# Pauses, order and place: the chain of tiles 1 and 2 beside gathered expert rows in a hybrid decoder step

## The reference, cut to what matters

```
h  = modulate(rms_norm(x));  z = h @ w_in
o  = [sparse attention (compressed, selected, window) | causal pooling mixer]
x1 = x + gate1 * (o @ w_out)
h2 = modulate(rms_norm(x1))
q  = h2 @ peer_wq;  s = q . peer_subkeys        # 8 heads, two sets of 128 keys
eid, g = top16 of the 16 x 16 sums; g = softmax # 128 experts for each token
a  = gelu(h2 . peer_u[eid])
y  = x1 + gate2 * sum_k (g * a)_k peer_v[eid_k]
```

## Time and profile before

| | us |
|---|---|
| median of three runs | 2595.06 |
| the profiled execution's own time | 2596.01 |
| its span in the trace | 2594.2 |
| VectorE busy | 1758.1 (68%) |
| TensorE busy | 1273.0 (49%) |
| GpSimd busy | 1111.4 (43%) |
| ScalarE busy | 212.3 (8%) |
| first row of tile 0's dots / sums | 600.8 / 1048.9 |
| first row of tile 1's dots / sums | 1562.4 / 1902.6 |
| start of the looped phases | 2256.4 |

### The profile page before, as it was taken

How to read it: one execution, slowest core, us unless ns; L and a number is a source line. 1 busy time by engine, 2 the same in 40 slices (tenths; PEclk the granted TensorE clock), 3 DMA queues, 4 the chain that set the end, 5 groups by cost and what they waited for, 6 DMA issues and landing times.

```text
span 2594.2 us, 17761 instructions
## 1 busy us (share of the span) xinstructions
PE 1273.0 (49%) x6317; PEld 690.3 (27%) x6317; DVE 1758.1 (68%) x2243; ACT 212.3 (8%) x559; POOL 1111.4 (43%) x686
## 2 busy tenths in 40 slices
PE   4699998896680542456866961000035466200000
PEld 2363534582230531343323930000012122000000
DVE  1010112226968977996558668999999967899897
ACT  3110013100010221121001011000000000000000
POOL 1000100002434744674124312688853455788684
PEclk9699899898795555566985975555566767655555
DMA  9949899759999989999998989999999999999897
GB/s 296 329 178 422 321 420 277 225 191 382 389 419 397 378 359 347 412 411 343 338 397 319 418 310 392 355 422 422 422 401 340 349 408 416 422 422 422 368 422 302
DMA packets 163041, 944.47 MB, mean 364 GB/s; under 512 B 34635, under 2 KB 44435, under 8 KB 56830
## 3 DMA queue, kind: packets, MB, share of 16 engines
q0 software_dynamic: 94784, 682.66, 65.8%
q1 hardware_dynamic: 68175, 260.74, 28.0%
HBM read 937.36 MB, written 10.26 MB: 365 GB/s over the span
## 4 chain that ended last, share of the span: by engine, by line
DVE 25%; PE 24%; DMA 22%; POOL 16%; issue 9%; SPq 2%; ACT 1%; POOLq 0%; DVEq 0%; ACTq 0%
POOL arena L668 11%; DMA arena<-in_peer_u,arena 10%; DVE arena L1994 7%; DVE arena L1971 6%; POOL arena L680 5%; DMA arena<-in_w_out 5%; DMA arena<-in_peer_v,arena 5%; PE PS L1445 3%; PE PS L1016 3%; DMA arena<-in_w_ada 3%; PE PS L1166 2%; PE PS L966 2%; PE PS L1253 2%; PE PS L1468 2%; PE PS L1070 2%
## 5 line engine op out<-in xcount | busy, mean ns | idle before, releaser
L1971 DVE CUSTOM_DVE_ANT_0 arena<-arena 128x2048 f32<-128x2048 f32 x256 | 582.3, 2289 | 117.6 <-DMA arena<-in_peer_u,arena 116.2
L668 POOL DMA_INDIRECT arena<-in_peer_u,arena x256 | 441.3, 1724 | 475.3 <-DVE arena L1971 275.9
L1994 DVE SCALAR_TENSOR_TENSOR arena<-arena 128x2048 f32<-128x2048 f32 x226 | 530.9, 2349 | 159.8 <-DMA arena<-in_peer_v,arena 155.1
L668 POOL DMA_INDIRECT arena<-in_peer_v,arena x256 | 379.7, 1483 | 442.2 <-DVE arena L1994 329.1
L1468 PE MATMUL PS<-arena 128*128 128x512 f32 x240 | 177.7, 909 | 476.3 <-DMA arena<-in_peer_v,arena 400.7
L1468 PEld LDWEIGHTS PS<-arena 128*128 128x128 f32 x240 | 68.6, 300 | 586.1 <-issue 499.9
L1474 PE MATMUL PS<-arena 128*64 128x512 f32 x8 | 5.9, 903 | 345.7 <-DVEq L2037 345.7
L2027 DVE SCALAR_TENSOR_TENSOR arena<-arena 128x2048 f32<-128x2048 f32 x64 | 150.5, 2352 | 11.3 <-DMA arena<-in_peer_v,arena 5.6
L966 PE MATMUL PS<-arena 128*32 128x512 f32 x768 | 123.2, 741 | 69.4 <-DMA arena<-in_w_ada 66.1
L2024 DVE CUSTOM_DVE_ANT_0 arena<-arena 128x2048 f32<-128x2048 f32 x64 | 144.9, 2289 | 8.1 <-DMA arena<-in_peer_u,arena 6.3
L680 POOL DMA_INDIRECT arena<-in_peer_v,arena x64 | 132.8, 2075 | 35.2 <-issue 19.2
(11 more groups left out here) (347 smaller groups left out, 1812.7 us busy)
## 6 DMA issues: line engine op xcount, KB each, us to landing
arena<-in_w_ada SPq DMA_DIRECT2D x96, 1024.0 KB, 12.0
arena<-in_w_in SPq DMA_DIRECT2D x32, 1048.0 KB, 10.2
arena<-in_peer_wq SPq DMA_DIRECT2D x32, 1024.0 KB, 9.9
arena<-in_w_in SPq DMA_DIRECT2D x32, 768.0 KB, 11.6
arena<-in_w_out SPq DMA_DIRECT2D x16, 1024.0 KB, 30.3
arena<-in_w_out SPq DMA_DIRECT2D x32, 512.0 KB, 23.6
arena<-in_peer_u,arena POOLq DMA_INDIRECT x320, 13.9
arena<-in_peer_v,arena POOLq DMA_INDIRECT x320, 13.4
```

The costliest lines, as they stand in the source:

```text
L668: pool.indirect_dma_start(out=rows_ring[:, k % NROW, :], out_offset=None, in_=tables[kind], in_offset=bass.IndirectOffsetOnAxis(ap=ids[:, ...
L1971: V.tensor_tensor_reduce(out=buf, in0=buf, in1=h2(t), scale=1.0, scalar=0.0, op0=ALU.mult, op1=ALU.add, accum_out=dots[:, t, r:r + 1]).the ...
L1994: V.scalar_tensor_tensor(out=acc[t], in0=rows_ring[:, k % NROW, :], scalar=dots[:, t, r:r + 1], in1=acc[t], op0=ALU.mult, op1=ALU.add).the ...
```

## The change

The pauses are cut (12, 20, 3, 20, 30 become 0, 2, 3, 4, 20, and the one ahead of the second addition is three times the one ahead of the first). In `beside_dots` most other pauses between steps become one row; an attention unit has three yields in place of four. Sample attention moves from `beside_sums` into `beside_dots`, with three yields a sample in place of six. `paced(work, n)` puts n yields after each step of a generator: the second expert half of tile 1 moves into tile 0's sums (2 rows a step), the first half of tile 2 into tile 1's dots (3 rows a step), and the second half of tile 2 stays in tile 1's sums (2 rows a step). `expert_exp` takes one half at a time, and ScalarE has them at other places; `gelu(0)` goes behind sample attention and the gate's evictions. TensorE spreads the first gate for both column halves before the products of the output projection, over all eight banks, in place of one half at a time.

```diff
-Q_PAUSE, K_PAUSE, S_PAUSE, OUT_PAUSE, WQ_PAUSE = 12, 20, 3, 20, 30
+Q_PAUSE, K_PAUSE, S_PAUSE, OUT_PAUSE, WQ_PAUSE = 0, 2, 3, 4, 20
@@ ScalarE
-            def expert_exp(t):
-                for half in range(2):
-                    w = gw[:, t, half * HH:(half + 1) * HH]
-                    act.wait_ge(s_e2, 2 * t + half + 1)
-                    A(w, w, exp).then_inc(s_e2x, 1)
+            def expert_exp(t, half):
+                w = gw[:, t, half * HH:(half + 1) * HH]
+                act.wait_ge(s_e2, 2 * t + half + 1)
+                A(w, w, exp).then_inc(s_e2x, 1)
...
-            expert_exp(0)
+            expert_exp(0, 0)
...
                 A(qkr[:, 1:3, NH:24], qkr[:, 1:3, NH:24], sqrt).then_inc(s_zrt, 1)
+            expert_exp(0, 1)
...
-            gelu(0)
...
-                        A(GB_12[h][:, k, m * SECTION:(m + 1) * SECTION], PS[:, 4 + 2 * k + m, :], copy).then_inc(s_gb, 1)
+                        A(GB_12[h][:, k, m * SECTION:(m + 1) * SECTION], PS[:, 4 - 4 * h + 2 * k + m, :], copy).then_inc(s_gb, 1)
+            gelu(0)
             norm2(1)
...
             chunk_out(5)
+            expert_exp(1, 0)
...
-            expert_exp(1)
+            expert_exp(1, 1)
+            expert_exp(2, 0)
             gelu(1)
-            expert_exp(2)
+            expert_exp(2, 1)
@@ TensorE
-                        last = spread(4 + 2 * k + m, 2, 2 * h + m, selT[:, k, :])
+                        last = spread(4 - 4 * h + 2 * k + m, 2, 2 * h + m, selT[:, k, :])
                 last.then_inc(s_gp, 1)
-                if h == 1:
-                    pe.wait_ge(s_gb, 12)
+            pe.wait_ge(s_gb, 12)
+            for h in range(2):
...
-                pe.wait_ge(s_gb, 8)
@@ VectorE
+            def paced(work, n):
+                for _ in work:
+                    yield from pause(n)
@@ beside_dots
-                yield from pause(4)
+                yield
                 cmp_shift(1, 6)
-                yield from pause(2)
+                yield
...
-                yield from pause(3)
+                yield
                 cmp_norm(1)
-                yield from pause(4)
+                yield
                 p_max(8)
                 for u in range(8, 16):
                     yield
+                    p_norm(u)
                     yield
-                    p_norm(u)
                     if u < 15:
-                        yield
                         p_max(u + 1)
                     yield
-
-            def beside_sums():
-
                 yield from pause(S_PAUSE)
                 dve.wait_ge(s_bs, 32)
                 dve.wait_ge(s_gsi, 16 * NH)
                 s_max(0)
                 for b in range(DB):
-                    yield from pause(2)
+                    yield
                     smp_norm(b)
+                    yield
                     if b + 1 < DB:
-                        yield from pause(2)
                         s_max(b + 1)
-                    yield from pause(2)
+                    yield
+
+            def beside_sums():
+
                 for h in range(2):
-                    yield from pause(OUT_PAUSE)
+                    yield from pause(OUT_PAUSE * (2 * h + 1))
                     yield from add1(h)
...
                 yield from pause(WQ_PAUSE)
                 yield from experts(1, 0)
+                yield from paced(experts(1, 1), 2)
 
             def beside_dots1():
-                yield from experts(1, 1)
-                yield from pause(2)
+                yield from paced(experts(2, 0), 3)
                 shares(1)
@@ beside_sums1
-                for half in range(2):
-                    yield from experts(2, half)
+                yield from paced(experts(2, 1), 2)
                 yield from pause(2)
```

## The result

The changed kernel takes 2657.59 us (median of four runs, 2652.2 to 2665.52) against 2595.11 us: a ratio of 1.0241, 95% interval 1.0223 to 1.0259, 62.5 us slower. I had forecast 2621, 26 us slower, with a range of 2573 to 2658. The sign was right; the loss was 2.4 times the one forecast.

The account below looks back on a forecast made before the run. DMA queues bound the kernel wherever VectorE keeps up. Losing 32 us through sample attention and 34 to tile 0's end, regaining 40 in tile 1, gave 26 us: 2621, own range 2603 to 2640, with rivals 2573 to 2658.

Parts of the forecast that it names:

- 92 MB of other loads: All loads behind 600 us other than the gathered rows, sized by their shapes: 219 us at 422 GB/s.
- Gain 1: ScalarE's new order removes TensorE's 46.0 us wait before the input projection's second half; it ends at 726, not 768.7.
- Loss 1: Up to the attention units: VectorE waits 13 and 6.6 us; units start at 800 after 41 rows, not 884 after 80.
- Loss 2: Attention units with three rows, not four: 9.9 us each, DMA idling some 19 us in 24 rows.
- Loss 3: Sample attention: late biases and pages, then steps with nothing spare; it ends at 1014 with 95 rows, 32 us lost.
- first-page wait: Start of sample attention: VectorE waits about 20 us because the first value pages queue behind two pieces of w_out.
- a ring of 13.5: Sample attention: each sample's chain of dependent steps across engines takes 13.5 us, against 9.3 us of VectorE work.
- the rows hide the ring: Rival in sample attention: a sample goes at VectorE's 9.3 us and the first wait goes; 2578 us, chance 0.27.
- the pages set it: Rival in sample attention: page loads make each sample 18.7 us in place of 13.5; +36, 2657 us, chance 0.15.
- To the end of tile 0's sums: From sample attention's end to tile 1's dots: a further 34 us lost, dots starting at 1628, 66 us later.
- Gains 2 and 3: Fewer expert steps beside tile 1: dots 325 us against 340, sums 329 against 354, together 40 us back.
- The sum: Whole kernel: 32 + 34 - 40 = 26 us slower, 2621 us against 2595.1.

Follow-up runs that it names:

- a_win100: Changed kernel with the large copy (win_sample, 3968 KB) left at row 100 and the small one (pool_sample, 224 KB) issued at row 300: 2651.10 us.

## Why the prediction was right or wrong

**The step that failed** is "the output projection's loads share the queues with 34 rows in 155 us; after it is the same, so they end at 1169 with row 129". They ended at 1189 with row 128. The term was mis-sized: from the end of sample attention to the last product it took 183 us (1006 to 1189), not 155, and only that sample attention ended 8 us ahead of my 1014 hides a part of it. I took the stage's duration from the trace of before and left out what else stands on POOL's queue: 4.3 MB of copies, tied to row 100 and not to the stage. My 92 MB of other loads lack them too (the trace has 96.7 MB beside the rows behind 600 us). The change moved row 100 from the attention units to the start of this stage. Without the copies there, the products take 142 to 145 us; the time falls by 22 us with the copies at row 300 or on SyncE's queue, and by 31 with them at row 88. The prediction's remark that the halves of w_out move slowly was right, and it was not followed up.

**Gain 1** was right in the size of the wait (2.9 us are left of 46), and it was not a gain by itself: in the kernel before, the new order costs 5 us; with the short pauses it is worth 26.

**Loss 1** was too large by 10 us: units at 790 where I had 800. 7 of them are in the waits, 7.4 and 5.2 us where I had 13 and 6.6.

**Loss 2** was right: 9.9 us a unit with three rows.

**Loss 3** was right in the lost DMA time, and only roughly in its parts. I had a first-page wait of 20 us, a ring of 13.5 and the end at 1014 with 95 rows; it was 25.9, 13.3 and 1006. The DMA time not filled up to the end of sample attention, time less bytes at 422 GB/s, is 73.0 us after and 40.9 before: 32 us lost, as forecast, though I had 62 and 30. In a_smp6, with six rows a sample, the unfilled time up to 1048 us is 50.4, so most of the loss is the three rows'. The rival in which the rows hide the ring fell, as did the one in which the pages set it.

**To the end of tile 0's sums**: 90 us late where I had 66. 21 of the 24 are the failed step (row 128 at 1188 where it was to be at 1167), 3.5 came behind it. The wait for the scores was 49 us (forecast 46), the second half 6.0 us for two rows as forecast; TensorE's wait for the second addition was 64.0 us.

**Gains 2 and 3** were 12 and 22 us, not 15 and 25: dots of 328 us (325 forecast), sums of 331 (329). In the dots, the first 66 rows took 172.5 us (174 forecast), the other 62 took 155.6. My 148 for these was too low even by my own 2.49 us a row, which gives 154.

**The sum.** On the profiled spans 2650.0 against 2620 (2594.2 and 26): 21 up to row 128, which is the output projection's stage, 3.5 from row 128 to 256, 5.5 from tile 1. The rest of the error, some 6 us, is that the median lies 5.4 us above the profiled execution, where in the kernel before it lay 0.9 below. The forecast's own range ended at 2640. That the wider range, up to 2658, held the time was luck: its upper end is the bound of a rival that did not occur.

**Open**: why transfers are slower while halves of w_out land, and whether the eight lagging parts are what keeps the low rate up to some 1150 us, long after the large copy has ended. That the copy's place causes it is shown by moving it; how it does so is my reading of the traces. A copy cut so that it spreads like the other loads was not run.

## What to carry to other kernels

When a change moves steps from row to row, list everything that is tied to a row number on every queue, and ask what each now stands beside. Pauses count in rows, waits in microseconds: a chain that is cut short in rows only helps if no step waits, and here three more rows a sample, five ahead of the first addition, twelve before the scores and another place for the copies turned 62 us lost into 25 won. A wait that only moves on when its transfer is issued earlier, as with the value pages, points to a bound in bytes. A full DMA share does not say that the bytes move at the full rate: look at GB/s beside it.

## What the runs showed of the hardware

The large copy from HBM to HBM, 3968 KB, holds the gathers behind it on its queue up by 12.8 us among attention units, 26.6 beside loads of w_out, 14.1 to 19.4 at row 300. It runs as 64 packets with mostly eight under way at a time, and takes 20 us in the kernel before and 22 in the changed one.

The same gathers and w_out loads, at a full DMA share and with the same packet sizes, move at about 420 or about 275 GB/s for tens of microseconds at a time. An 8 KB packet of the gathers then takes some 315 or some 490 ns. The lower rate stands while loads for 64 partitions land (276 to 299 GB/s in the four kernels of the table). While loads for 128 partitions land it is 406 to 420, but 281 and 291 with the large copy just ahead of them (changed kernel, a_win100).
